# A two-word matmul chain: the 512-column matmul of a weight-stationary tile becomes two of 256 columns into the same PSUM columns

## What is computed

```python
h = _rmsnorm(x, norm_mix)
proj = einsum('bsd,de->bse', h, w_in)            # 2048 -> 4096: b, c, xt, v, 1024 each
y_conv = b * causal_depthwise_conv3(c * xt)
y_pool = scale * per_group_linear(trailing_mean(v) - v)   # 4 groups of 256 x 256
x = x + einsum('bse,ed->bsd', concat(y_conv, y_pool), w_out)      # 2048 -> 2048
u = relu(einsum('bsd,df->bsf', _rmsnorm(x, norm_mlp), w_up))      # 2048 -> 8192
x = x + einsum('bsf,fd->bsd', u * u, w_down)                      # 8192 -> 2048
return _rmsnorm(x, norm_final)
```

## Time and profile before

| | |
|---|---|
| Median of three runs | 1005.84 us |
| Profiled execution, its own time | 1005.23 us |
| Its span, first to last instruction | 1003.4 us |
| TensorE busy | 991.5 us, 5088 matmuls, 5088 weight loads |
| VectorE busy | 586.3 us |
| ScalarE busy | 419.5 us |
| Mean granted TensorE clock | 0.997 |

### The profile page before, as it was taken

The page is one execution under the profiler, slowest core; times in us unless marked ns, Lnnn a source line. Parts: engine busy times, 40 slices in busy tenths (PEclk is TensorE's granted clock), DMA queues, the critical chain, the costliest instruction groups (busy, mean ns, idle before and its releaser), DMA issues.

```text
span 1003.4 us, 12457 instructions
## 1 busy us (share of the span) xinstructions
PE 991.5 (99%) x5088; PEld 844.3 (84%) x5088; DVE 586.3 (58%) x428; ACT 419.5 (42%) x325; POOL 1.4 (0%) x9
## 2 busy tenths in 40 slices
PE   8999999999999999999999999999999999999996
PEld 7888888888888888888888888888888888888885
DVE  6596768655565656454656654456565455656453
ACT  6744434454444434333343433343433334434342
POOL 0000000000000000000000000000000000000000
PEclk9999999999999999999999999999999999999998
DMA  9956544555544645555454555545545554555512
GB/s 330 388 205 225 199 167 144 192 220 200 173 170 173 239 169 208 179 197 201 163 201 188 188 189 206 175 160 209 201 179 208 177 200 136 207 203 208 186 66 84
DMA packets 29694, 193.52 MB, mean 193 GB/s; under 512 B 3296, under 2 KB 3552, under 8 KB 7136
## 3 DMA queue, kind: packets, MB, share of 16 engines
q1 hardware_dynamic: 29232, 190.85, 51.8%
q10 hardware_dynamic: 288, 1.18, 0.3%
q0 software_dynamic: 144, 1.05, 0.3%
HBM read 190.97 MB, written 2.10 MB: 192 GB/s over the span
## 4 chain that ended last, share of the span: by engine, by line
PE 98%; DMA 1%; DVE 0%; ACT 0%; SPq 0%; ACTq 0%; issue 0%
PE ps L323 43%; PE ps L256 36%; PE ps L258 17%; PE ps L255 1%; DMA w_raw<-w_stream 1%; PE ps L309 0%; PE ps L297 0%; SPq L193 0%; ACT cross L463 0%; ACT x L600 0%; DVE x L907 0%; DVE w_lo L703 0%; ACT w_hi L490 0%; ACTq L55 0%; SPq L208 0%
## 5 line engine op out<-in xcount | busy, mean ns | idle before, releaser
L608 DVE TENSOR_TENSOR w_lo<-w_raw,w_hi 128x2048 fp32r<-128x2048 f32 x172 | 392.1, 2291 | 284.8 <-ACT w_hi L429 284.1
L256 PE MATMUL ps<-act_a,w_hi 128*128 128x512 f32 x1536 | 540.8, 398 | 2.8 <-DVE w_lo L703 2.8
L429 ACT ACTIVATE w_hi<-w_raw 128x2048 fp32r<-128x2048 f32 x172 | 327.0, 1913 | 350.0 <-PE ps L323 210.8
L258 PE MATMUL ps<-act_a,w_lo 128*128 128x256 f32 x1440 | 404.1, 281 | 0.0
L256 PEld LDWEIGHTS ps<-act_a,w_hi 128*128 128x128 f32 x1536 | 287.3, 188 | 71.8 <-DVE w_lo L703 3.3
L323 PE MATMUL ps<-w_hi,act_b 128*128 128x512 f32 x1280 | 345.0, 389 | 0.0
L323 PEld LDWEIGHTS ps<-w_hi,act_b 128*128 128x128 f32 x1280 | 240.1, 188 | 49.7
L258 PEld LDWEIGHTS ps<-act_a,w_lo 128*128 128x128 f32 x1440 | 272.0, 189 | 0.9
L323 PE MATMUL ps<-w_lo,act_b 128*128 128x512 f32 x640 | 199.7, 389 | 0.0
L323 PEld LDWEIGHTS ps<-w_lo,act_b 128*128 128x128 f32 x640 | 120.1, 188 | 24.9
L615 DVE TENSOR_TENSOR val<-ps,cross 128x1024 f32<-128x1024 f32 x26 | 31.8, 1224 | 49.3 <-ACT cross L435 49.3
(11 more groups left out here) (64 smaller groups left out, 147.9 us busy)
## 6 DMA issues: line engine op xcount, KB each, us to landing
w_raw<-w_stream SPq DMA_DIRECT2D x172, 1024.0 KB, 4.8
w_raw<-w_stream SPq DMA_DIRECT2D x16, 256.0 KB, 8.1
x<-x_rows SPq DMA_DIRECT2D x2, 1024.0 KB, 16.9
mix_mem<-x_t SPq DMA_DIRECT2D x3, 512.0 KB, 8.5
out<-x SPq DMA_DIRECT2D x6, 256.0 KB, 2.7
mix_mem<-pool_w ACTq DMA_DIRECT2D x1, 1024.0 KB, 9.4
mix_mem<-g_final POOLq DMA_DIRECT2D x1, 1024.0 KB, 4.8
out<-val SPq DMA_DIRECT2D x2, 256.0 KB, 2.1
```

The lines of the kernel that those rows point to most:

```text
L256: mm = pe.matmul(ps[:, bank, :], weights_hi, act, start=first, stop=last)
L258: mm = pe.matmul(ps[:, bank, 0:S], weights_lo, act[:, 0:S], start=False, stop=False)
L429: act.activation(w_hi[:, c, :], w_raw[:, c, :], ACT.Copy).then_inc(hi_ready, 1)
L608: dve.tensor_tensor(out=w_lo[:, c, :], in0=w_raw[:, c, :], in1=w_hi[:, c, :].bitcast(F32), op=ALU.subtract)\
```

## The change

`pair` becomes `three`: the high weights by the high words, the high weights by the low words, the low weights by the high words, each 256 columns wide and all into the first 256 columns of the bank. The same order holds at every k step. The second halves of the banks are not used by these tiles any more, so `take_cross` and `cross_ready` go. VectorE waits for the chunk count itself (for `pool_done` in the pool jobs) and copies the four sums to `val`. ScalarE's program keeps its splits and high words in their order, without the copies.

```diff
-        def bank_halves(parity, half):
-            return ps[:, NT * parity:NT * parity + NT, half * S:(half + 1) * S]
+        def bank_halves(parity):
+            return ps[:, NT * parity:NT * parity + NT, 0:S]
...
-            def pair(bank, weights_hi, weights_lo, act, first, last):
-                if last:
-                    pe.matmul(ps[:, bank, 0:S], weights_lo, act[:, 0:S], start=False, stop=False)
-                mm = pe.matmul(ps[:, bank, :], weights_hi, act, start=first, stop=last)
-                if not last:
-                    mm = pe.matmul(ps[:, bank, 0:S], weights_lo, act[:, 0:S], start=False, stop=False)
-                return mm
+            def three(bank, weights_hi, weights_lo, act, first, last):
+                to = ps[:, bank, 0:S]
+                pe.matmul(to, weights_hi, act[:, 0:S], start=first, stop=False)
+                pe.matmul(to, weights_hi, act[:, S:2 * S], start=False, stop=False)
+                return pe.matmul(to, weights_lo, act[:, 0:S], start=False, stop=last)
...
-            def take_cross(t, parity):
-                if not (isinstance(t, int) and t == 0):
-                    act.wait_ge(summed, t)
-                act.activation(cross[:, :, :], bank_halves(parity, 1), ACT.Copy).then_inc(cross_ready, 1)
-            def take_block(n, parity):
-                act.wait_ge(chunk_used, 4 * n + 4)
-                take_cross(turn(n), parity)
...
-            def add_halves(t, parity, crosses):
-                dve.wait_ge(cross_ready, crosses)
-                dve.tensor_tensor(out=val[:, :, :], in0=bank_halves(parity, 0),
-                                  in1=cross[:, :, :], op=ALU.add).then_inc(summed, 1)
+            def take(t, parity):
+                dve.tensor_copy(out=val[:, :, :], in_=bank_halves(parity)).then_inc(summed, 1)
                 dve.wait_ge(summed, t + 1)
+            def take_block(n, parity):
+                dve.wait_ge(chunk_used, 4 * n + 4)
+                take(turn(n), parity)
...
             for j in range(POOL_JOBS):
-                add_halves(POOL_AFTER + j, j, POOL_AFTER + j + 1)
+                dve.wait_ge(pool_done, j + 1)
+                take(POOL_AFTER + j, j)
```

More of the change, by code:

```diff
@@ L29 @@
 HALVES = S // P
-IN_CROSSES = IN_BLOCKS + POOL_JOBS
 POOL_AFTER = 6
@@ L114, in build @@
         chunk_used = sem("chunk_used")
-        cross_ready = sem("cross_ready")
         summed = sem("summed")
@@ L265, in products @@
                     at = BLOCK_COLS * k + P * nt
-                    mm = pair(NT * (t % 2) + nt, w_hi[:, c, at:at + P], w_lo[:, c, at:at + P],
-                              src[:, kt, :], kt == 0, kt == KT - 1)
+                    mm = three(NT * (t % 2) + nt, w_hi[:, c, at:at + P], w_lo[:, c, at:at + P],
+                               src[:, kt, :], kt == 0, kt == KT - 1)
                 return mm
@@ L347, in pool_job @@
                             at = S * kc + P * dt
-                            mm = pair(bank, pool_hi[:, g, at:at + P], pool_lo[:, g, at:at + P],
-                                      act_b[:, 2 * g + kc, :], kc == 0, kc == 1)
+                            mm = three(bank, pool_hi[:, g, at:at + P], pool_lo[:, g, at:at + P],
+                                       act_b[:, 2 * g + kc, :], kc == 0, kc == 1)
                 mm.then_inc(pool_done, 1)
@@ L429, in split, with section @@
                 act.activation(w_hi[:, c, :], w_raw[:, c, :], ACT.Copy).then_inc(hi_ready, 1)
-            def take_cross(t, parity):
-                if not (isinstance(t, int) and t == 0):
-                    act.wait_ge(summed, t)
-                act.activation(cross[:, :, :], bank_halves(parity, 1), ACT.Copy).then_inc(cross_ready, 1)
-            def take_block(n, parity):
-                act.wait_ge(chunk_used, 4 * n + 4)
-                take_cross(turn(n), parity)
-            def section(n, before_last=None, parity=1):
+            def section(n, before_last):
                 for c in range(CHUNKS - 1):
                     split(n, c)
-                if before_last:
-                    take_block(n - 1, parity)
-                    before_last()
+                before_last()
                 split(n, CHUNKS - 1)
-            def nothing():
-                pass
             def act_b_hi(values, k0):
@@ L508, in diff @@
                    .then_inc(diff_hi, 1)
-            take_block(0, 0)
             split(2, 0)
@@ L518, in _ @@
             diff(0)
-            take_block(1, 1)
             split(2, 3)
@@ L525, in _ @@
             split(3, 2)
-            take_block(2, 0)
             split(3, 3)
-            section(4, nothing, 1)
+            for c in range(CHUNKS):
+                split(4, c)
             diff(3)
-            section(5, nothing, 0)
+            for c in range(CHUNKS):
+                split(5, c)
             for c in range(CHUNKS - 1):
                 split(6, c)
-            take_block(5, 1)
             for j in range(POOL_JOBS):
-                act.wait_ge(pool_done, j + 1)
-                take_cross(POOL_AFTER + j, j)
                 act.wait_ge(summed, POOL_AFTER + j + 1)
@@ L544, in _ @@
                     split(6, CHUNKS - 1)
-            section(7, act_b_hi(1, 8), 0)
-            section(8, act_b_hi(2, 12), 1)
+            section(7, act_b_hi(1, 8))
+            section(8, act_b_hi(2, 12))
             for j in range(OUT_BLOCKS):
@@ L569, in up_down @@
                 for j in range(3):
-                    section(n + (1 + j), act_b_hi(4 * p + (3 + j), NT * j), j % 2)
-                section(n + 4, act_b_hi(4 * p + 6, NT * 3), 1)
+                    section(n + (1 + j), act_b_hi(4 * p + (3 + j), NT * j))
+                section(n + 4, act_b_hi(4 * p + 6, NT * 3))
                 for j in range(3):
@@ L576, in _ @@
             weights(n + 1)
-            take_block(n, 0)
             take_spread(1)
@@ L580, in _ @@
             for j in range(1, 4):
-                section(n + (1 + j), act_b_hi(3 + j, NT * j), j % 2)
+                section(n + (1 + j), act_b_hi(3 + j, NT * j))
             for j in range(3):
@@ L610, in split, with section @@
                    .then_inc(lo_ready, 1)
-            def add_halves(t, parity, crosses):
-                dve.wait_ge(cross_ready, crosses)
-                dve.tensor_tensor(out=val[:, :, :], in0=bank_halves(parity, 0),
-                                  in1=cross[:, :, :], op=ALU.add).then_inc(summed, 1)
+            def take(t, parity):
+                dve.tensor_copy(out=val[:, :, :], in_=bank_halves(parity)).then_inc(summed, 1)
                 dve.wait_ge(summed, t + 1)
-            def section(n, before_last, parity, crosses):
+            def take_block(n, parity):
+                dve.wait_ge(chunk_used, 4 * n + 4)
+                take(turn(n), parity)
+            def section(n, before_last, parity):
                 for c in range(CHUNKS - 1):
                     split(n, c)
-                add_halves(turn(n - 1), parity, crosses)
+                take_block(n - 1, parity)
                 before_last()
@@ L754, in take_v @@
                 times_inv_rms(j + 1, v[:, NT * j:NT * j + NT, PAD:PAD + S])
-            add_halves(0, 0, 1)
+            take_block(0, 0)
             split(2, 0)
@@ L769, in _ @@
             diff_lo(0)
-            add_halves(turn(1), 1, 2)
+            take_block(1, 1)
             take_v(1)
@@ L827, in b_block @@
                 return go
-            add_halves(turn(2), 0, 3)
+            take_block(2, 0)
             c_block(0)()
             split(3, 3)
-            section(4, c_block(1), 1, 4)
+            section(4, c_block(1), 1)
             diff(3)
             diff_lo(3)
-            section(5, xt_block(0), 0, 5)
+            section(5, xt_block(0), 0)
             for c in range(CHUNKS - 1):
                 split(6, c)
-            add_halves(turn(5), 1, 6)
+            take_block(5, 1)
             take_xt(1)
             for j in range(POOL_JOBS):
-                add_halves(POOL_AFTER + j, j, POOL_AFTER + j + 1)
+                dve.wait_ge(pool_done, j + 1)
+                take(POOL_AFTER + j, j)
                 dve.wait_ge(act_hi_ready, j + 1)
@@ L850, in _ @@
             convolve(1)
-            section(7, b_block(0), 0, IN_CROSSES - 1)
-            section(8, b_block(1), 1, IN_CROSSES)
+            section(7, b_block(0), 0)
+            section(8, b_block(1), 1)
             for t in range(HALVES):
@@ L880, in _ @@
                 split(n + 1, c)
-            add_halves(turn(n), 0, IN_CROSSES + 1)
+            take_block(n, 0)
             dve.wait_ge(inv_rms_ready, 2)
@@ L884, in _ @@
             for j in range(1, 4):
-                section(n + (1 + j), up(0, j), j % 2, IN_CROSSES + j + 1)
+                section(n + (1 + j), up(0, j), j % 2)
             for j in range(3):
@@ L891, in _ @@
                 for j in range(4):
-                    section(n + (1 + j), up(p, j), j % 2, 4 * p + (IN_CROSSES + j + 1))
```

(1 more changed line is left out.)

## The result

The changed kernel takes 1017.66 us (1017.29 to 1017.67) against 1005.48 us for the kernel before in the same session; the ratio is 1.0119, 95% interval 1.0107 to 1.0132. The medians differ by 12.2 us, which is what was forecast (the ratio, with its interval, gives 10.8 to 13.3 us). The profiled executions differ by 12.4 us (1017.67 against 1005.23), and their spans by 12.5 (1015.9 against 1003.4).

The account below looks back on a forecast made before the run. TensorE's instruction stream, busy for 99% of the span, was taken as the bound. Longer tiles add 12.2 us, all else 0: 1005.84 + 12.2 = 1018.0 us, with 1002 to 1028 as the range for 8 in 10.

Parts of the forecast that it names:

- step 1: TensorE tile: three 256-column matmuls, each with a covered weight load, at 120 ns; 360 ns a tile, bounds 340 to 366.
- step 3: TensorE's stream: the longer tiles summed over all blocks and pool jobs, +12.2 us on 1552 tiles; row blocks untouched.
- Step 2: TensorE accumulating into the same 256 columns without a 512-column matmul between: costs nothing; 1 ns would be 3 us.
- Steps 4 and 5: Block take-out: dropping ScalarE's 26 cross copies gains 0; VectorE's copy replaces its add at about 1224 ns, also without effect.
- Step 6: TensorE issue: six instructions per tile in 360 ns, one each 60 ns, taken to cost nothing.
- Rival A: TensorE: a 256-column matmul costs what its spacing reads, about 117 ns; -3.3 us, 1002.5 us; chance 0.17.
- B: TensorE: the second matmul with the same weights is cheaper, 346.3 ns a tile; -9.0 us, 996.8 us; chance 0.05.
- E: TensorE: repeated weights spare part of the fixed cost, 354.9 ns a tile; +4.3 us, 1010.1 us; chance 0.06.
- D: TensorE's sequencer can't issue six instructions in 360 ns; 372 ns a tile, +30.8 us, 1036.6 us; chance 0.06.
- C: TensorE: 20 of 24 blocks keep the slow rate's extra 6.1 ns a tile; 7.8 us on top, 1025.8 us; chance 0.18.

Follow-up runs that it names:

- grouped order: The kernel before with each k step issuing four 512-column matmuls, one for each tile, then the four of 256 columns: 1002.93 us, ratio 0.9974.

## Why the prediction was right

Steps 1 and 3, the price of a matmul and the sum, held: 120.0 ns a matmul, 360.0 ns a tile, four up blocks 1.78 us longer where 4 x 0.45 was forecast, the whole 12.2 us by the medians. The fixed part came out at 13.3 ns, not 13.7, which the column price made up for. The load had 8 ns to spare, not 11: the floor in long streams is 111 to 112 ns, not the 109 of the transposes. In step 3 the first up block's +0.9 is 0.98 by its own figures (23.04 - 22.06), 0.1 us in the sum. The profiled span is 0.3 us over the sum, and 0.28 of that can be put down to the second weight piece: the first unbroken stretch of matmuls began at 10.38 us instead of 10.10, with the wait for the pieces at 2.5 us in all. The method that worked was to take two sums from the trace with different numbers of matmuls and columns, 226.7 and 346.9 ns, and solve for a fixed part and a part per column. The runs at 384 and 512 columns confirm both parts from 256 columns up; at 240 the line no longer holds. The choice of the fast block (346.9) over the common one (353.0) for the solving is what made the answer come out at 120 rather than at 126; it was supported only by the column price landing on 2.4 GHz, and the common one would have forecast some 40 us more instead of 12. The choice was in part a guess, which the runs bore out.

Step 2: accumulating into the same columns costs nothing, as the run with the cross half kept shows.

Steps 4 and 5: the run with only the new way of taking out came out the same as before. VectorE's copy takes 1223 ns, the add took 1224. After the change VectorE waits for TensorE (30.4 us in all) where it waited for ScalarE (49.3 us). No matmul waits for a block to be taken out: TensorE's only waits are those before 10.4 us.

Step 6: six instructions in 360 ns pass without a hole; the 192-column run sustains two in 111 ns.

Rival A was the reading of single spacings. The spacing after a narrow matmul reads 117 ns on average where widths take turns, and 120.0 where all are narrow, so it was no price. In the clean block of the kernel before the other spacing makes up for it (start us, us, instruction):

```profile
154.95 0.28 PE L258 MATMUL ps<-act_a,w_lo 128*128 128x256 f32 x1
155.06 0.39 PE L256 MATMUL ps<-act_a,w_hi 128*128 128x512 f32 x1
...
155.99 0.28 PE L258 MATMUL ps<-act_a,w_lo 128*128 128x256 f32 x1
156.10 0.39 PE L256 MATMUL ps<-act_a,w_hi 128*128 128x512 f32 x1
```

Three tiles take 1.04 us, 346.7 ns each. In the trace's ns the spacings are 117 after a narrow and 230 after a wide matmul, tile after tile. That is what 120.0 and 226.7 would read if the start of the wide one were stamped 3.3 ns early; that it is stamped early is a reading, not shown. At the slow rate they are 117 and 236 on average. Only sums over whole tiles are prices. B fell by the equal spacings behind equal and changed weights, E with it. D fell by the absence of holes. The Trainium skill (TensorE: Matmul & The Clock Gate, Back-to-back issue gap) gives N/2.4 + 2.5 ns, as the gap of a single matmul by itself. The price of a column is the one measured here; the fixed part is not: 13.3 ns fits 256, 384 and 512 columns, each with its own fp32r weight load.

C, the slower rate kept, fell as well, and the reason given in step 1 ("uniform streams run at the clean rate") turned out right: in every long run of one width the extra 6.3 ns a tile are gone. Taking turns costs 353.0 a tile, a change each four matmuls 350.6 (grouped order, 552.37 - 462.61 us for 256 tiles), each 32 matmuls 347.3; two of 384, with turns left only in the first and last k step, 347.1 (549.22 - 460.37 us). The change removed this surcharge and paid 13.3 ns for it: 353.0 - 6.3 + 13.3 = 360.0. Without that hidden gain it would have cost 20 us.

What stays open is why some blocks of the kernel before ran clean although widths took turns there (149.79 to 171.99 in the earlier trace rows). It isn't the place in the program, since that block ran at 353.1 ns a tile in the run with only the new way of taking out. Nor is a change of width a fixed price: per change the surcharge is 0 in those blocks, 3.2 ns where widths take turns at the slow rate, some 8 in runs of four and some 10 in runs of 32. The mechanism wasn't found.

## What to carry to other kernels

Where TensorE has no idle time, count matmuls as well as columns: each fp32r matmul of 256 columns or more, with its weight load, cost 13.3 ns beyond its columns here, so splitting a wide one to save another engine's copy pays only if that engine is on the path. Solve for the two parts from two sums over many instructions, not from spacings between single ones. When matmuls of two widths share a stream, try long runs of one width: runs of 32 took 7.2 us off this kernel.

## What the hardware showed

Within a stream of fp32r matmuls, each with its load, the spacing was 226.7 ns at 512 columns, 173.6 at 384 and 120.0 at 256, at granted clock 1.00. What part of the 13.3 ns beyond the columns is the matmul's and what the load's, no run separates. At 240 columns it was 112.0 ns and at 192 it was 111 to 112 ns, so narrower than 240 columns saved next to nothing (985.7 and 984.83 us, one run each). Not expected: a stream in which 512 and 256 columns take turns ran at 353.0 ns a pair over most blocks, 6.3 ns above the sum of its parts, in either order of the neighbours in a bank, and with ScalarE's copies or without them.
